# Every weight tile of an expert as a split product, with three buffers of high parts, and a gather that no longer stands behind a scatter

## The reference

```python
def expert_choice(h, w_router, w_gate, w_up, w_down):
    ...
    vals, idx = lax.top_k(jnp.swapaxes(aff, 1, 2), cap)
    xs = h[bidx, idx]
    hid = jax.nn.silu(jnp.einsum('becd,edf->becf', xs, w_gate)) * jnp.einsum('becd,edf->becf', xs, w_up)
    y = jnp.einsum('becf,efd->becd', hid, w_down) * vals[..., None].astype(h.dtype)
    return jnp.zeros_like(h).at[bidx, idx].add(y)
```

## Time and profile before

| | us |
|---|---|
| median of three runs (2896.15 to 2900.72) | 2896.93 |
| time of the profiled execution | 2899.66 |
| its span | 2897.9 |
| TensorE busy | 2740.6 |
| VectorE busy | 1696.3 |
| ScalarE busy | 1409.8 |
| from the first expert's transposes to the last output, in the trace | 925 to 1516 |

### The profile page before, as it was taken

One profiled execution on the slowest core, in us unless ns is written; L12 is line 12 of the kernel. 1 busy time (PEld: TensorE's weight loads), 2 busy tenths in 40 slices (PEclk: granted clock), 3 DMA queues, 4 the chain that ended last, 5 costly groups with the idle time before them and its releaser, 6 DMA issues.

```text
span 2897.9 us, 38375 instructions
## 1 busy us (share of the span) xinstructions
PE 2740.6 (95%) x13959; PEld 2053.2 (71%) x13959; DVE 1696.3 (59%) x3159; ACT 1409.8 (49%) x2564; POOL 212.7 (7%) x245
## 2 busy tenths in 40 slices
PE   8999999999993999999998998999999999999898
PEld 4578795888772777777766865776678876876686
DVE  2378372343467888888865568555643656546533
ACT  3343262232252766666656456645632557447421
POOL 0100000000010000000006000000020000000500
PEclk9999999999996999999998999999999999999999
DMA  9610301223344999999975200210041301000321
GB/s 377 214 58 30 115 3 58 88 88 116 133 151 176 339 376 377 377 376 378 377 236 175 39 15 8 59 44 30 16 146 60 116 1 60 30 19 20 117 87 58
DMA packets 178458, 401.60 MB, mean 139 GB/s; under 512 B 7948, under 2 KB 9004, under 8 KB 177792
## 3 DMA queue, kind: packets, MB, share of 16 engines
q1 hardware_dynamic: 158224, 329.27, 32.0%
q0 software_dynamic: 19936, 70.26, 7.5%
q10 hardware_dynamic: 144, 0.01, 0.0%
HBM read 363.70 MB, written 35.81 MB: 138 GB/s over the span
## 4 chain that ended last, share of the span: by engine, by line
PE 83%; DVE 8%; ACT 4%; issue 2%; DMA 2%; DVEq 0%; POOLq 0%; SPq 0%; POOL 0%; ACTq 0%
PE psum L303 10%; PE psum L805 7%; PE psum L807 7%; PE psum L806 7%; PE psum L1529 4%; PE psum L1527 4%; PE psum L1528 4%; PE psum L1684 4%; PE psum L1472 3%; PE psum L1471 3%; PE psum L1470 3%; PE psum L1702 3%; PE psum L1726 3%; PE psum L1804 2%; PE psum L1805 2%
## 5 line engine op out<-in xcount | busy, mean ns | idle before, releaser
L806 PE MATMUL psum<-ring_r,cols_r 128*128 128x512 f32 (+1 forms) x544 | 212.1, 390 | 0.0
L806 PE MATMUL psum<-ring_r,kctx_r 128*128 128x512 f32 (+1 forms) x544 | 210.3, 387 | 0.0
L2228 ACT ACTIVATE ring<-ring,att 128x256 f32<-128x256 f32 (+7 forms) x256 | 173.2, 677 | 19.4 <-DVE att L2919 19.3
L2770 DVE TENSOR_TENSOR ring_r<-ring,pair_r 128x1024 fp32r<-128x1024 f32 x128 | 148.0, 1217 | 50.6 <-ACT pair_r L2100 50.6
L1684 PE MATMUL psum<-wide 64*128 64x512 f32 (+2 forms) x704 | 148.2, 501 | 5.8 <-DVE att L2919 2.8
L1528 PE MATMUL psum<-ring_r,wide_r 128*128 128x512 f32 x384 | 151.2, 394 | 0.0
L642 DVE TENSOR_TENSOR ring_r<-ring,ring_r 128x1024 fp32r<-128x1024 f32 x48 | 58.7, 1225 | 129.7 <-ACT ring_r L639 129.2
L1470 PE MATMUL psum<-small_r,ring_r 128*128 128x512 f32 x320 | 125.8, 393 | 0.8 <-DVE pair L2640 0.8
L1472 PE MATMUL psum<-small_r,ring_r 128*128 128x512 f32 x320 | 126.3, 395 | 0.0
L2100 ACT ACTIVATE pair_r<-ring 128x1024 fp32r<-128x1024 f32 x128 | 124.4, 1045 | 0.6 <-PE psum L1529 0.6
L1702 PEld LDWEIGHTS psum<-ident,ring 128*128 128x128 f32 x640 | 67.9, 141 | 73.7 <-issue 41.5
(11 more groups left out here) (571 smaller groups left out, 7139.7 us busy)
## 6 DMA issues: line engine op xcount, KB each, us to landing
ring<-in_w_gate SPq DMA_DIRECT2D x64, 1024.0 KB, 9.2
ring<-in_w_up SPq DMA_DIRECT2D x32, 1024.0 KB, 10.4
hidden<-in_w_up SPq DMA_DIRECT2D x32, 1024.0 KB, 9.9
hidden<-in_w_down SPq DMA_DIRECT2D x32, 1024.0 KB, 8.1
pair<-in_w_down SPq DMA_DIRECT2D x30, 1024.0 KB, 9.5
ring<-in_w_ada SPq DMA_DIRECT2D x24, 1024.0 KB, 13.9
ring<-in_w_in SPq DMA_DIRECT2D x24, 1024.0 KB, 7.3
ring<-in_even_w_in SPq DMA_DIRECT2D x16, 1024.0 KB, 12.2
```

Of the source, the lines that this page charges most:

```text
L806: self.eng.matmul(outp, XHIGH[b][:, k, :], low[:, k, 0:wd], start=False, stop=False)
```

## The change

- All six tiles are split (`MSPLIT = 6`), and both tiles of `last_down`.
- `MHIGH` has three buffers, tile j uses number j % 3 (`moe_high`), and `moe_high_free` waits for the product of tile j - 3. Each piece is 1024 columns wide; the new buffer lies in `wide`, `extra`, `cols` and `small`.
- No float32 copy of the hidden layer is made: `h_evac` is gone, ScalarE rounds each half straight out of PSUM and VectorE subtracts straight out of PSUM (`h_high`, `h_low`).
- `x_evac` is ScalarE's alone from expert 1 on.
- `high` of tiles moves ahead of `silu` by one place, and tiles 0 and 1 of the next expert are rounded in that order.
- GpSimd waits for the landing of scatter e - 1 just before it issues scatter e, no longer behind it.

```diff
                                      split["hidden"][:, SLOT:2 * SLOT], split["pair"][:, 0:SLOT])]
-        MHIGH = [[tile_of(split["pair"][:, SLOT:2 * SLOT])[:, 0:4, :], tile_of(split["pair"][:, SLOT:2 * SLOT])[:, 4:8, :]],
-                 [tile_of(split["ctx_hidden"][:, 0:2 * D]), tile_of(split["small"][:, 0:2 * D])]]
+        MHIGH = [[tile_of(v) for v in views] for views in
+                 ([split["pair"][:, SLOT + i * D:SLOT + (i + 1) * D] for i in range(PIECES)],
+                  [split["ctx_hidden"][:, 0:D], split["ctx_hidden"][:, D:2 * D], split["small"][:, 0:D], split["small"][:, D:2 * D]],
+                  [split["wide"][:, 4 * D:5 * D], split["extra"][:, 0:D], split["cols"][:, 0:D], split["small"][:, 3 * D:4 * D]])]
         XSH, XSL = split["wide"][:, 7 * D:8 * D], split["wide"][:, 8 * D:9 * D]
-        MSPLIT = 5
+        MSPLIT = 6
         HDH, HDL = split["sel_wT"][:, 0:D], split["small"][:, 2 * D:3 * D]
-        MPLACE = (1, 0, 2, 3, 4)
...
+        def moe_high(e, j):
+            return MHIGH[(j + 2 * int(isinstance(e, int) and e == 0)) % 3]
...
         def moe_high_free(eng, e, j):
-            first = isinstance(e, int) and e <= 1
-            if first and e == 0 and j < 2:
-                return
-            if j >= 2:
-                eng.wait_ge(S(("moe_g", "moe_u")[j // 2 - 1]), e * 2 + (j % 2 + 1))
-            elif j == 1 or first:
-                eng.wait_ge(S("moe_u"), e * 2 + (j - 1))
+            if isinstance(e, int) and e == 0:
+                if j == 3:
+                    eng.wait_ge(S("moe_g"), 1)
+            elif j == 5:
+                eng.wait_ge(S("moe_u"), e * 2 + 1)
+            elif j >= 3:
+                eng.wait_ge(S("moe_g"), e * 2 + (j - 2))
+            elif isinstance(e, int) and e == 1:
+                eng.wait_ge(S(("moe_g", "moe_u")[(j + 1) // 2]), (2, 1, 2)[j])
+            elif j == 0:
+                eng.wait_ge(S("moe_u"), e * 2)
             else:
-                eng.wait_ge(S("moe_d"), e * 2 - 3)
+                eng.wait_ge(S("moe_d"), e * 2 + (j - 4))
         HIGHS = split["ring"][:, 2 * SLOT:3 * SLOT].rearrange("p (k n) -> p k n", k=KT)
...
+                if not isinstance(e, int) or e >= 2:
+                    pool.wait_ge(S("moe_sct"), e * 16 - 16)
                 if more:
                     pool.tensor_copy(rows, idxc[:, bass.ds(e - 1, 1)])
                     pool.drain()
                 pool.indirect_dma_start(scratch["acc"], bass.IndirectOffsetOnAxis(rows.bitcast(U32), 0), yb, None,
                                         compute_op=ALU.add).then_inc(S("moe_sct"), 16)
-                pool.wait_ge(S("moe_sct"), e * 16)
-            with pool.Fori(1, NEXP - 1) as e:
+            one(1, True)
+            with pool.Fori(2, NEXP - 1) as e:
                 one(e, True)
             one(NEXP - 1, False)
...
-            def split_product(e, j, xh, xl, outp):
-                low, q = MLOW[j], j % 2
...
                     if k % PK == 0:
                         pe.wait_ge(S("mw_low"), moe_pieces(e, j) + (k // PK + 1))
-                    high = MHIGH[q][k // 4][:, k % 4, :]
+                    high = moe_high(e, j)[k // PK][:, k % PK, :]
                     pe.matmul(outp, xh[:, k, :], high, start=(k == 0), stop=False)
...
             def down(e):
-                pe.wait_ge(S("moe_hlow"), e + before("moe_hlow"))
-                split_product(e, 4, hdh, hdl, bank(4)).then_inc(S("moe_d"), 1)
-                moe_full(pe, e, 5)
-                group(pe, bank(5), [(hidT[:, k, :], MRAW[5][:, k, :]) for k in range(KT)]).then_inc(S("moe_d"), 1)
+                for j in (4, 5):
+                    split_product(e, j, hdh, hdl, bank(j)).then_inc(S("moe_d"), 1)
...
             def last_down():
-                pe.wait_ge(S("moe_y"), 2 * NEXP - 3)
...
-                mm.then_inc(S("moe_d"), 1)
+                pe.wait_ge(S("moe_hlow"), 2 * NEXP + before("moe_hlow"))
+                for m in range(2):
+                    pe.wait_ge(S("moe_y"), 2 * NEXP - 3 + m)
+                    split_product(NEXP, m, hdh, hdl, bank(4 + m), MLOW[2 + m]).then_inc(S("moe_d"), 1)
...
             def turn(e, more):
                 pe.wait_ge(S("moe_sil"), e * 2)
                 pe.wait_ge(S("moe_hid"), e * 2)
                 gate_up(e)
+                pe.wait_ge(S("moe_hlow"), e * 2 + before("moe_hlow"))
                 if more:
-                    pe.wait_ge(S("moe_hevA"), e)
-                    pe.wait_ge(S("moe_hevD"), e)
                     x_transposes(e + 1)
                 if not isinstance(e, int) or e >= 2:
                     pe.wait_ge(S("moe_y"), e * 2 - 2)
...
             def x_evac(e):
-                act.wait_ge(S("moe_xtr"), e * 2 + 1)
-                for k in range(4):
-                    ins = act.activation(xsT[:, k, :], bank(6)[:, span(k)], ACT.Identity, bias=adaT[:, 3 * KT + k:3 * KT + k + 1],
+                for k in range(4 if isinstance(e, int) and e == 0 else KT):
+                    if k % 4 == 0:
+                        act.wait_ge(S("moe_xtr"), e * 2 + (k // 4 + 1))
+                    ins = act.activation(xsT[:, k, :], bank(6 + k // 4)[:, span(k % 4)], ACT.Identity, bias=adaT[:, 3 * KT + k:3 * KT + k + 1],
                                          scale=mod[:, 2 * KT + k:2 * KT + k + 1])
                 ins.then_inc(S("moe_xevA"), 1)
...
@@ -2096,17 +2090,19 @@
                 moe_full(act, e, j)
                 moe_high_free(act, e, j)
                 for p in range(PIECES):
-                    ks = slice(PK * p, PK * (p + 1))
-                    act.activation(MHIGH[j % 2][p // 2][:, PK * (p % 2):PK * (p % 2 + 1), :], MRAW[j][:, ks, :], ACT.Copy).then_inc(S("mw_high"), 1)
...
+            def last_high(m):
+                last_full(act, 2 + m)
+                act.wait_ge(S(("moe_u", "moe_d")[m]), 2 * NEXP - 3 * m)
+                for p in range(PIECES):
+                    act.activation(moe_high(NEXP, m)[p], MRAW[2 + m][:, PK * p:PK * (p + 1), :], ACT.Copy).then_inc(S("mw_high"), 1)
             def h_high(e):
-                act.wait_ge(S("moe_hevA"), e + 1)
-                act.wait_ge(S("moe_hevD"), e + 1)
-                act.activation(HDH, hd, ACT.Copy).then_inc(S("moe_hhigh"), 1)
+                for h in range(2):
+                    act.wait_ge(S("moe_htr"), e * 2 + (h + 1))
+                    act.activation(HDH[:, h * HALF:(h + 1) * HALF], bank(6 + h), ACT.Copy).then_inc(S("moe_hhigh"), 1)
...
             def turn(e, more):
                 act.wait_ge(S("moe_hid"), e * 2)
+                high(e, 2)
                 silu(e, 0)
-                high(e, 2)
+                high(e, 3)
                 silu(e, 1)
-                high(e, 3)
                 high(e, 4)
+                high(e, 5)
                 if more:
                     x_evac(e + 1)
                     x_high(e + 1)
+                    high(e + 1, 0)
                     high(e + 1, 1)
-                    high(e + 1, 0)
                 else:
-                    last_full(act, 5)
-                    act.wait_ge(S("moe_u"), 2 * NEXP)
-                    for p in range(PIECES):
-                        ks = slice(PK * p, PK * (p + 1))
-                        act.activation(MHIGH[1][p // 2][:, PK * (p % 2):PK * (p % 2 + 1), :], MRAW[2][:, ks, :], ACT.Copy).then_inc(S("mw_high"), 1)
-                h_evac(e)
+                    last_high(0)
+                    last_high(1)
                 h_high(e)
-            with act.Fori(1, NEXP - 1) as e:
+            turn(1, True)
...
-            def low(e, j):
...
             def h_low(e):
-                dve.wait_ge(S("moe_hhigh"), e + (1 + before("moe_hhigh")))
-                dve.tensor_tensor(HDL, hd, HDH.bitcast(F32), ALU.subtract).then_inc(S("moe_hlow"), 1)
+                for h in range(2):
+                    hs = slice(h * HALF, (h + 1) * HALF)
+                    dve.wait_ge(S("moe_hhigh"), e * 2 + (h + 1 + before("moe_hhigh")))
+                    dve.tensor_tensor(HDL[:, hs], bank(6 + h), HDH[:, hs].bitcast(F32), ALU.subtract).then_inc(S("moe_hlow"), 1)
...
             def turn(e, more):
                 low(e, 2)
                 low(e, 3)
+                low(e, 4)
                 dve.wait_ge(S("moe_htr"), e * 2)
                 hidden_of(e, 0)
-                low(e, 4)
+                low(e, 5)
                 hidden_of(e, 1)
                 if more:
-                    x_evac(e + 1)
                     x_low(e + 1)
-                    low(e + 1, 1)
+                    low(e + 1, 0)
+                else:
+                    low(NEXP, 0, 2)
                 if not isinstance(e, int) or e >= 2:
                     dve.wait_ge(S("moe_sct"), e * 16 - 16)
-                if not more:
-                    for p in range(PIECES):
-                        ks = slice(PK * p, PK * (p + 1))
-                        dve.wait_ge(S("mw_high"), moe_pieces(NEXP, 1) + (p + 1))
```

(4 more changed lines are left out.)

64 lines of the change are left out of this document (22 added, 42 removed).

## The result

The changed kernel takes **3002.57 us** (median of five runs, 2996.88 to 3006.75) against 2896.93: a ratio of 1.0354, 95% interval 1.0343 to 1.0366. It is 3.5% slower where I had forecast 0.3% faster, and far outside the range. The profiled execution took 2999.97, 100.3 more than the one of before.

A forecast was written before the change was run, and what follows sets the result against it. TensorE sets today's pace; after the change the DMA, 36.16 us a turn against TensorE's 34.90, would bound. Summed over the DMA, rounding, products and clock, output starts at 1506.7 instead of 1515.41: 8.7 us gained, 2888.2 us, range 2880 to 2893.5.

The forecast's parts named there:

- The gather* follows the scatter at once: GpSimd in each expert's turn: gather issued right behind the scatter, not waited for by TensorE's transposes; priced at nothing.
- Three buffers ... this alone buys nothing: Rounded high parts: made 11 us ahead of need instead of 5.5; no gain alone, but makes room for the sixth tile.
- turns of 34.91 us: TensorE among the experts: a split product saves 1.27 us, so turns take 34.90 us at first, later 36.2.
- the wait ahead of `last_down`: End of the experts: TensorE waits some 6 us after its transposes for data and low parts.
- the clock behind it: TensorE after its wait at the end: lower clock costs 2.1 us, bounds 0 and 5.6.
- the last output at 1506.08: End of the experts: last output starts at 1506.7 instead of 1515.41, a gain of 8.7 us.
- the store: Weight tiles landing early, 16.4 us ahead; 11 to 14 us usable, letting TensorE outrun the DMA for nine to eleven turns.
- the clock's upper bound: TensorE in `last_down`: the lower clock costs at most 5.6 us, taken as all of it at half speed.
- The second rival: End of the experts: 5.6 us lost to the clock and a DMA lead of 0.9 leave 2892.6 us; chance 0.20.
- Slower: Rival: gather meets scatter in the full DMA, 1.15 us more on each of 14 turns, 2904.3 us; chance 0.07.
- The DMA has more to give: Rival: loads run faster than 386 GB/s and TensorE stays the bound; gain 18.8 us, time 2878.1; chance 0.12.
- No change: Rival: no difference that can be told, under 0.2% or 5.8 us, time 2892.6; chance 0.20.

The follow-up runs named there:

- e2: The kernel before with only GpSimd's part of the change, the gather issued without a wait for the scatter's landing; 2897.86 us, ratio 0.9997.
- e5: The kernel before, no wait for the scatter's landing, GpSimd's loop written out without copies and drains; 2900.32 us, ratio 1.0005.
- e3: The changed kernel with the gather of expert e + 2 issued ahead of the turn's scatter; 2891.45 us, ratio to the kernel before 0.9976.
- e1: The changed kernel with GpSimd's wait for the landing of scatter e put back right behind it; 3006.29 us, ratio to the kernel before 1.0369.
- e6: The changed kernel with GpSimd's loop written out, no copies and no drains; 2920.64 us, ratio to the kernel before 1.0078.
- e4: The changed kernel with weights' low parts replaced by raw copies through one-input `tensor_reduce`; 2892.75 us, ratio to the kernel before 0.9979.
- e14: The kernel before plus four needless one-input reductions a turn on VectorE between `h_evac` and `h_low`; 2898.18 us, ratio 0.9999.
- e7: The changed kernel with VectorE pausing before a turn's low parts until GpSimd is through the scatter; 2937.10 us, ratio to the kernel before 1.0133.
- e8: The changed kernel with ScalarE, from turn 2 on, waiting for the product two tiles back, not three; 2947.97 us, ratio to the kernel before 1.0174.
- e11: The kernel before with only GpSimd's order changed, gather of expert e + 2 ahead of the scatter; 2897.97 us, ratio 1.0000.
- e13: The kernel before plus four needless two-input subtractions a turn on VectorE between `h_evac` and `h_low`; 2943.62 us, ratio 1.0157.

## Why the prediction was wrong

**The step that failed** is "*The gather* follows the scatter at once. It is used at the transposes, which don't wait for it today. Priced at nothing." It cost 87.7 us of waits and some 24 behind them. "Don't wait today" was no measure of room: from the end of `down` to the landing of the gather the turn was full to 2.1 us, and I had not laid that chain out. Nor had I given the scatter a length that could change; it went from 1.6 to 10.5 us, and the gather is issued 14.9 to 24.3 us behind it. "At once" was wrong even with a fast scatter: 9.4 us (e2), since the copy and the drain stand between (1.9 without them, e5).

**"Three buffers ... this alone buys nothing"** priced VectorE by its sum, 32.6 of 34.9, and the sum was right: 32.49 in the turn of e3 above. But the third buffer lets that work close up into runs of 20 us of two-input subtractions, and a transfer that GpSimd issues into such a run is held (changed kernel, e1, e3, e6); with one input (e4, e14), with a pause at its issue (e7) or without the buffer's lead (e8) it isn't, or by 1.1 us at most. The gap in which the scatter was issued is gone with `h_evac`, and the last output comes 2.3 us later behind `down` (e4). The sum of each of the three engines was under the turn; what VectorE does to GpSimd stood in none of them.

**Right, as e3 shows**, once the gather is off the path: turns of 34.91 us (forecast 34.90); ScalarE 30.17 a turn (29.1); DMA share 1.05; the last w_down of expert 14 at 1473.7 (1477.4) and the very last half tile at 1484.6 (1486.5); the wait ahead of `last_down` 8.55 (6), since `h_low` comes last; the clock behind it, 13.85 us to the last output instead of 11.2, so 2.6 (2.1), at 0.50 over the first 3.8 us; the last output at 1506.08 (1506.7). A gain of 6.9 us (0.24%; the interval gives 4.1 to 9.9), forecast 8.7. Off in detail: the store lasts for twelve turns of 34.9 us and one of 35.5, where I had said nine to eleven, and the landing times grow from 7.6 us in turn 2 to between 14 and 19, and no further.

**Slips in the working**, which did not decide anything. The strips of the earlier trace rows have 376 to 378 GB/s in six of the seven slices, not five. And the clock's upper bound, "5.6, which is all of `last_down` at half speed", is half of that: 11.2 us of products at half speed cost 11.2 more. The second rival, which needed 5.6, therefore asked for the low level over half of `last_down` only, not throughout; e3 measured 2.6.

**The rivals.** "Slower" had the sign, at a chance of 0.07, by a mechanism that did not occur: I let gather and scatter meet in a full DMA, but in the changed kernel the gather is issued when the scatter has landed, and the DMA fell to some 320 GB/s and moved nothing from 1208 to 1212. In e5, where they do go out 1.9 us apart, nothing is lost (ratio 1.0005). "The DMA has more to give" is not borne out by e3. One of its turns has 381 GB/s, but over the eleven turns from 979.6 to 1363.65 it moved 375, against 374 in the kernel before (979.6 to 1436): TensorE's shorter turns lived on the store, and the last tiles came too late for it by the 8.55 us. "No change" is what e2 and e11 give for GpSimd's order alone.

**Two inputs and GpSimd's port.** Two-input `tensor_tensor` held a scatter for up to 15 us (e3), one-input instructions did not (e4, e14). The Trainium skill, "SBUF — State Buffer", section "Who interferes with whom", has GpSimd's only SBUF port pair shared with VectorE, says that a VectorE instruction with two SBUF inputs contends with a GpSimd instruction that reads SBUF, and puts a DMA that VectorE stalls down to GpSimd being starved at writing descriptors; looked up before, it would have pointed to this place. By its rule on reads the runs agree: the rows show that both transfers read their row numbers from SBUF (`kctx`). But the same section reports `tensor_tensor` as not stalling a DMA, and infers that it takes only the read interface, while the writing of descriptors needs the write interface. For these indirect transfers the runs differ from that. Which side they were held at, no run shows.

**Open.** What lets the transfer out. Often it ends 1.4 to 1.6 us behind the start of an instruction of VectorE with an input in PSUM (in e3 at 1186.8, behind 1185.20), or behind a gap. But in the turn shown it ended at 1187.8, in e13 at 1163.8 and in e8 at 1159.0, each 1.5 to 1.6 us behind the start of a plain two-input subtraction (1186.24, 1162.30, 1157.46), with no gap in the records, while other such starts let nothing out. So "VectorE's gaps" is too simple an account of how the third buffer's lead makes the scatter long. Which part of a transfer is held, whether `tensor_tensor` with one SBUF input and a constant would be as harmless as `tensor_reduce`, and that it is the drain and not the copy that waits in e2, was not tried apart.

## What to carry to other kernels

Before pricing a step on a side engine at nothing, lay out its whole chain from what releases it to its use, and write down the room: here it was 2.1 us. When VectorE is made denser, look for indirect DMAs issued by GpSimd: put them where VectorE is idle or has at most one input in SBUF, or so early that a delay of 15 us doesn't matter. A wait taken out of a program gains only if nothing behind it (here a copy with a drain) waits for the same thing.

## What was not expected of the hardware

- A GpSimd indirect DMA of 1.6 us lasts 5.9 to 15.2 us, and lands in 18.5 in the median (23.5 at most) instead of 8.6, when it is issued into a run of VectorE subtractions with two SBUF inputs and nothing holds these up (changed kernel; likewise e1, e3); beside reductions with one input it doesn't (e4: 1.63 at most).
- A copy and a drain on GpSimd behind an indirect DMA hold the next one until it has landed: it is issued 9.4 us behind with them (e2), 1.9 without (e5).
- Scatters issued 0.5 and 0.7 us into the same run of VectorE take 2.2 and 6.5 us (e13).
